# Neighbourhood attention: the k-parts of the linear path in twos on the even steps

## The reference, cut to what matters

```python
h = rms_norm_2(x, norm_mix[l])
proj = h @ w_in[l]
na_q, na_k, na_v, r_q, r_k, r_v, r_g = jnp.split(proj, splits, axis=-1)
...
s = jnp.einsum('bcqhd,bicjhd->bhcqij', q_row, k_win).astype(F32) * scale
s = s + jnp.transpose(bias, (0, 2, 3, 1, 4))[None]
s = jnp.where(valid[None, None, :, :, None, :], s, NEG)
p = jax.nn.softmax(s.reshape(s.shape[:4] + (kh * band,)), axis=-1)
p = p.reshape(s.shape).astype(v.dtype)
return jnp.einsum('bhcqij,bicjhd->bcqhd', p, v_win)
```

## Time and profile before

| | us |
|---|---|
| median of three runs | 2437.14 |
| the profiled execution in all | 2437.95 |
| its span, first to last instruction | 2436.1 |
| TensorE (PE) busy | 2381.0 (98%) |
| TensorE weight loads (PEld) busy | 1877.6 (77%) |
| VectorE (DVE) busy | 1623.0 (67%) |
| ScalarE (ACT) busy | 1066.1 (44%) |
| GpSimd (POOL) busy | 943.0 (39%) |
| steps 0 to 7 of the four pairs begin at | 1337, 1392, 1446, 1501 |
| mean granted clock of TensorE, share of full | 0.995 |

### The profile page before, as it was taken

How to read it: one execution, slowest core, us unless ns; L and a number is a source line. 1 busy time by engine, 2 the same in 40 slices (tenths; PEclk the granted TensorE clock), 3 DMA queues, 4 the chain that set the end, 5 groups by cost and what they waited for, 6 DMA issues and landing times.

```text
span 2436.1 us, 31580 instructions
## 1 busy us (share of the span) xinstructions
PE 2381.0 (98%) x11548; PEld 1877.6 (77%) x11548; DVE 1623.0 (67%) x2013; ACT 1066.1 (44%) x1630; POOL 943.0 (39%) x528
## 2 busy tenths in 40 slices
PE   9999999999999999999999999999989999999997
PEld 6888648887777777776788777788868888788885
DVE  6999874467656466575866555445687777638985
ACT  5556572335544555446442333223344344443334
POOL 2899912332222122222233111222335555465554
PEclk9999999999999999999999999999999999999999
DMA  3111153221111111111032111221125666886773
GB/s 136 44 44 51 66 184 113 78 89 49 45 40 40 40 40 44 40 40 40 27 109 68 49 39 34 81 73 41 52 111 144 157 149 161 228 294 234 274 252 121
DMA packets 112228, 238.76 MB, mean 98 GB/s; under 512 B 42472, under 2 KB 45416, under 8 KB 112104
## 3 DMA queue, kind: packets, MB, share of 16 engines
q1 hardware_dynamic: 73152, 216.28, 27.6%
q10 hardware_dynamic: 38952, 20.76, 3.8%
HBM read 184.44 MB, written 46.27 MB: 95 GB/s over the span
## 4 chain that ended last, share of the span: by engine, by line
PE 82%; DVE 7%; ACT 3%; POOL 3%; issue 3%; ACTq 0%; DMA 0%; DVEq 0%; POOLq 0%; SPq 0%
PE ps_A L873 23%; PE ps_B L873 23%; PE ps_B L1378 9%; PE ps_A L1378 8%; PE ps_C L1378 4%; PE ps_D L1378 3%; POOL ta L795 1%; PE ps_C L893 1%; PE ps_B L966 1%; PE ps_B L1119 1%; PE ps_C L1011 1%; POOL accp L795 1%; PE ps_D L893 1%; PE ps_D L1011 1%; PE ps_D L1104 1%
## 5 line engine op out<-in xcount | busy, mean ns | idle before, releaser
L769 POOL CAST w_hi<-w_raw 128x1024 fp32r<-128x1024 f32 x98 | 107.9, 1101 | 1100.9 <-PE ps_A L873 476.8
L762 POOL TENSOR_TENSOR w_lo<-w_raw,w_hi 128x1024 fp32r<-128x1024 f32 x124 | 304.5, 2456 | 49.8 <-ACT w_hi L1518 41.9
L838 POOL TENSOR_TENSOR down_w_lo<-d_raw,down_w_hi 128x512 fp32r<-128x512 f32 x112 | 178.3, 1613 | 141.4 <-ACT down_w_hi L2201 141.4
L873 PE MATMUL ps_A<-HA_hi,w_hi 128*128 128x512 f32 x640 | 202.0, 397 | 4.7 <-POOL w_lo L762 2.2
L873 PE MATMUL ps_B<-HA_hi,w_hi 128*128 128x512 f32 x640 | 202.0, 397 | 1.6 <-POOL w_lo L762 1.6
L873 PE MATMUL ps_A<-HA_lo,w_hi 128*128 128x512 f32 x640 | 197.6, 390 | 0.0
L873 PE MATMUL ps_B<-HA_lo,w_hi 128*128 128x512 f32 x640 | 197.5, 390 | 0.0
L873 PE MATMUL ps_A<-HA_hi,w_lo 128*128 128x512 f32 x640 | 197.4, 390 | 0.0
L873 PE MATMUL ps_B<-HA_hi,w_lo 128*128 128x512 f32 x640 | 197.3, 390 | 0.0
L873 PEld LDWEIGHTS ps_A<-HA_hi,w_hi 128*128 128x128 f32 x640 | 117.3, 188 | 36.2 <-issue 10.9
L873 PEld LDWEIGHTS ps_A<-HA_lo,w_hi 128*128 128x128 f32 x640 | 120.1, 188 | 25.6
(11 more groups left out here) (489 smaller groups left out, 5938.6 us busy)
## 6 DMA issues: line engine op xcount, KB each, us to landing
w_raw<-w_dram SPq DMA_DIRECT2D x124, 512.0 KB, 3.3
d_raw<-w_dram SPq DMA_DIRECT2D x64, 512.0 KB, 4.5
t_raw<-u_dram SPq DMA_DIRECT2D x56, 512.0 KB, 5.8
a_raw<-w_dram SPq DMA_DIRECT2D x32, 512.0 KB, 7.7
u_dram<-b SPq DMA_DIRECT2D x56, 256.0 KB, 4.7
u_dram<-t SPq DMA_DIRECT2D x48, 256.0 KB, 7.0
X<-x_dram SPq DMA_DIRECT2D x16, 512.0 KB, 6.6
d_raw<-w_dram SPq DMA_DIRECT2D x32, 256.0 KB, 3.0
```

The lines of the kernel that those rows point to most:

```text
L762: pool.tensor_tensor(w_lo[q][:, :, :], w_raw[q][:, :, :], w_hi[q][:, :, :].bitcast(F32), ALU.subtract).then_inc(S[f"w_ready{q}"], 1)
L769: pool.tensor_copy(w_hi[q][:, :, :], w_raw[q][:, :, :]).then_inc(S["w_rounded"], 1)
L838: pool.tensor_tensor(lo[:, :, :], d_raw[i % 3][:, down_parts(x), :], hi[:, :, :].bitcast(F32), ALU.subtract).then_inc(S["down_split"], 1)
L873: op = pe.matmul(AB[b][:, cols], wt[:, w0 + k, :], act[:, k, cols], start=(first and k == ks[0] and step == 0), stop=(last and k == ks[-1] ...
```

## The change

In the neighbourhood part, TensorE's program does the k-parts u and u+1 of the fourth tile in front of the scores of every even unit u, and none in front of the scores of odd units. The `lin_done` of the tile is raised by k-part 7 as before, which now stands in step 6. All other instructions, waits and their order are unchanged, on TensorE and on the other engines; the results are the same.

```diff
@@ -1045,8 +1045,10 @@
                 tile = take_ab()
                 other = tile ^ 1
                 for u, (cb, half) in enumerate(NA_BLOCKS):
-                    op = products(tile, q, HB, [u], first=(u == 0), last=(u == KT - 1))
-                    if u == KT - 1:
+                    if u % 2 == 0:
+                        op = products(tile, q, HB, [u], first=(u == 0), last=False)
+                        op = products(tile, q, HB, [u + 1], first=False, last=(u == KT - 2))
+                    if u == KT - 2:
                         op.then_inc(S[f"lin_done{q}"], 1)
                     if u == 0:
                         pe.wait_ge(S[f"ab_free{other}"], n.now(f"ab_free{other}"))
```

## The result

The changed kernel takes 2446.61 us (median of six runs, 2445.64 to 2446.94); the kernel before, beside it, 2436.76. The ratio is 1.0039, with a 95% interval of 1.0029 to 1.0049: slower by 9.85 us on the medians, where +9.0 was forecast.

The account below looks back on a forecast made before the run. TensorE, busy 98% of the span, bounds the kernel, so its order and few waits count. Each pair grows by 2.26 us; four pairs add 9.0 to the median 2437.14, giving 2446.1 us, range 2442 to 2450.5.

Parts of the forecast that it names:

- The gate: Odd steps: values wait for ScalarE's copy of the turned probabilities until 3.93 us after the even scores, a 0.86 us stall.
- The second gate: Odd steps: the turn of unit u cannot start before VectorE's normalisation allows it, 4.20 us after the even scores.
- Rival (b): Odd steps: only the probabilities hold PE, not the copy; two steps take 7.74 us, total 2440; chance 0.06.
- rival (a): Odd steps: PE passes without a wait, so shape changes and today's small waits are saved; 2432.8 us; chance 0.05.
- The sum of a pair: One pair, first product to the next linear tile's first product: 32.47 us instead of 30.21, +2.26.
- The bounds: ScalarE's gate 0.1 us earlier or later over 16 odd steps makes 1.6 us; so 2444 to 2449 for the forecast case.
- The step on the other engines: ScalarE, VectorE and queues keep instructions and order; the earlier return of the weight buffer is worth nothing.
- The estimate for a change of shape that no row shows: Odd steps, transposes straight into scores: between nothing and 0.19 us, left out of the sum because the wait swallows it.
- the 3.0 us which the change was credited with: Product groups moved out of 16 odd steps save 0.19 us of shape changes each, if PE never waited.
- the small waits of before: Today's waits of 0.10 us before scores(0) and 0.23 in step 2, four times, 1.3 us in all.
- Rival (c): Short PE idles in odd steps lower the clock: 2468.5 us if each does, 2451.7 if one per pair; chance 0.04.
- Rival (d): Behind the part, a later wait makes up the delay; 2441.6 us if half is absorbed; chance 0.03.

Follow-up runs that it names:

- turn_first: Changed kernel, but in odd steps TensorE turns the probabilities of unit u-1 before the values of unit u-2; 2451.88 us, ratio 1.0059.
- dve_copy: Changed kernel, but VectorE instead of ScalarE copies the turned probabilities of units 1, 3 and 5, before it normalises; 2443.09 us, ratio 1.0025.
- the second trace: Profile of a repeat run of the changed kernel, with nothing altered; 2446.49 us, ratio 1.0040.

## Why the prediction was right, point by point

- **The gate.** "So values(u-1) can start at 3.93": measured 3.92, with the copy named as releaser. Made longer, it moved the values by its own growth (eight pieces, 4.32); taken off ScalarE, it moved them to 3.52.
- **The second gate**, 4.20 by the probabilities: 4.18 in turn_first. Rival (b), in which it alone counts, is excluded in the changed kernel by the waits on the copy. It is why rival (a) wasn't reached by either of two variants: turn_first only meets it earlier, and in dve_copy, where the copy is early, the normalisation ends later (4.29 instead of 4.13), and two steps are still 0.26 us above before.
- **The sum of a pair**: 32.41, 32.53 and 32.50 against 32.47 forecast; scores(2) 7.73 to 7.83 behind scores(0), against 7.76. (The bounds speak of the gate in 16 odd steps; in step 1 the turn waits for the probabilities, so the copy is the gate in 12.)
- **What was mis-sized, one.** The step on the other engines, "ScalarE, VectorE and their queues do the same instructions in the same order", priced ScalarE's issues at nothing. They are the same, but an issue that took 1.77 us was covered by the slack of the copy, and that cover was gone: 0.69 us in the second pair. Without it the four pairs have grown by 9.1 us, against 9.0 forecast. In the second trace, where that wait was 0.18 us longer than the others, they grew by 9.2 in all.
- **What was mis-sized, two.** "The estimate for a change of shape that no row shows (...) lies between nothing and 0.19 us": it is 0.17 (0.80 against 0.63). The wait swallowed it, as said, but it means that TensorE arrived at 3.24 and not 3.07, so the true stall is 0.68 and the recorded total of waits 7.8 us instead of 9 to 10. Above all it means that the 3.0 us which the change was credited with if nobody waited were not there: an odd step gives back 0.02 us, not 0.19. Rival (a) would have given 16 x 0.02, about 0.3 us (an estimate: step 1 has other neighbours, and its change was never seen without a wait), and the small waits of before, 1.3.
- **Rival (c), the clock**: 1.00 in all four parts with twelve idles of 0.6 us and more, and still 1.00 with those of 0.86 to 1.45 us in turn_first and in the changed kernel with eight pieces. The Trainium skill, page "TensorE: Matmul & The Clock Gate", section "A second HAM failure mode: psum-queue depth-cycling", would have had it swing; idles of 0.6 us in 8.3 didn't do it here. Where the clock did fall, at 1140 to 1180 us, ahead of the part, it differed between two executions of the same instructions, 0.87 and 0.96.
- **Rival (d)**: the delay was carried to the end as far as the runs can tell; the medians differ by 9.85 us and the four pairs by 9.8. From the end of the fourth pair to the end of the span the two traces of the changed kernel take 904.1 and 905.1 us, the trace of before 904.7: no part of the delay is seen to be made up there, but a microsecond would not show.

None of the kernels tried is faster than the one before.

## What to carry to other kernels

Work that stands between a producer and its consumer on a full engine is cover, even if it belongs to something else: before it is moved, time the chain behind the last instruction that the consumer depends on, engine by engine in program order, and compare it with what is left in between. What a merge of groups saves must be priced with the change of shape that it creates, not only with the one that it removes. And slack also hides irregular costs such as slow load issues, so a chain brought to zero slack pays for those too.

## What the runs showed of the hardware that was not expected

- Six transposes on TensorE take 0.63 us from their start to that of the next group if products with 512 columns follow, and 0.80 to 0.81 if scores (64 rows) or values (64 columns out) follow. Why was not tested.
- ScalarE's issue of two loads takes 0.81 us as a rule, but 1.0 to 1.9 in a few steps, several of which recur from trace to trace; a copy placed behind it waits for its end, even though the exponentials before it ran beside it. What makes it slow stayed open.
- A copy of 768 columns on ScalarE in eight pieces instead of one makes the wait for it only 0.42 us longer, 0.06 for each further piece; two copies of unlike size (0.78 us for 768, 0.99 for 1024 columns) had suggested 0.15.
